# The opening of a two-block transformer kernel in another order: first product ahead of the context's norm, scalings in pairs, context's squares added by GpSimd

## What is computed

```python
mod_x = (silu(c) @ w_mod[i] + b_mod[i])[:, None, :]
mod_c = silu(c_ctx) @ w_mod[i] + b_mod[i]
sh_x, sc_x, g_x = jnp.split(mod_x, 3, axis=-1)
sh_c, sc_c, g_c = jnp.split(mod_c, 3, axis=-1)
hx = rms_norm(x, norm_g[i]) * (1.0 + sc_x) + sh_x
hc = rms_norm(ctx, norm_g[i]) * (1.0 + sc_c) + sh_c
```

## Time and profile before

| | before |
|---|---|
| median of three runs | 1638.76 us |
| the profiled execution | 1637.41 us |
| its span | 1635.7 us |
| PE busy | 1551.2 us (95%) |
| DVE, ACT, POOL busy | 740.2, 623.5, 658.7 us |
| mean granted clock of TensorE | 0.977 |

### The profile page before, as it was taken

One profiled execution on the slowest core, in us unless ns is written; L12 is line 12 of the kernel. 1 busy time (PEld: TensorE's weight loads), 2 busy tenths in 40 slices (PEclk: granted clock), 3 DMA queues, 4 the chain that ended last, 5 costly groups with the idle time before them and its releaser, 6 DMA issues.

```text
span 1635.7 us, 25366 instructions
## 1 busy us (share of the span) xinstructions
PE 1551.2 (95%) x10018; PEld 1227.2 (75%) x10018; DVE 740.2 (45%) x1717; ACT 623.5 (38%) x1303; POOL 658.7 (40%) x640
## 2 busy tenths in 40 slices
PE   5999999999898999999998899999999999999997
PEld 3887777787687888787876687878878865655755
DVE  4344555555533434444355563443424454456033
ACT  4234444454532533334344453433322343333221
POOL 2534344444432533434344453525345344333252
PEclk8999999999899999999999899999999999999998
DMA  9111111110133222323231222212122212110221
GB/s 396 47 60 52 31 49 53 53 52 27 72 123 103 78 78 78 104 78 110 72 104 52 78 92 73 100 52 103 52 78 78 90 66 78 52 52 27 78 98 57
DMA packets 22438, 129.80 MB, mean 79 GB/s; under 512 B 2480, under 2 KB 2608, under 8 KB 8368
## 3 DMA queue, kind: packets, MB, share of 16 engines
q1 hardware_dynamic: 22176, 127.92, 21.9%
q10 hardware_dynamic: 144, 0.26, 0.1%
HBM read 126.08 MB, written 2.10 MB: 78 GB/s over the span
## 4 chain that ended last, share of the span: by engine, by line
PE 81%; DVE 8%; ACT 3%; POOL 3%; issue 3%; DMA 1%; SPq 0%; POOLq 0%; DVEq 0%; ACTq 0%
PE PS L1442 15%; PE PS L1444 14%; PE PS L1443 14%; PE PS L1565 6%; PE PS L1540 6%; PE PS L1523 4%; PE PS L1696 3%; PE PS L1437 3%; PE PS L1438 3%; PE PS L1439 3%; PE PS L1530 3%; DVE sm L2154 2%; PE PS L1706 2%; PE PS L1618 1%; PE PS L1610 1%
## 5 line engine op out<-in xcount | busy, mean ns | idle before, releaser
L2477 POOL TENSOR_TENSOR WL<-W,WH 128x512 fp32r<-128x512 f32 x280 | 367.4, 1328 | 321.7 <-ACT WH L1726 321.4
L1442 PE MATMUL PS<-HX,WH 128*128 128x512 f32 x1008 | 420.5, 417 | 11.3 <-DVE LX L2067 3.7
L1444 PE MATMUL PS<-HX,WL 128*128 128x512 f32 x1008 | 398.6, 395 | 0.0
L1443 PE MATMUL PS<-LX,WH 128*128 128x512 f32 x1008 | 398.3, 395 | 0.0
L1442 PEld LDWEIGHTS PS<-HX,WH 128*128 128x128 f32 x1008 | 192.5, 191 | 62.7 <-issue 17.9
L1444 PEld LDWEIGHTS PS<-HX,WL 128*128 128x128 f32 x1008 | 192.1, 191 | 42.7
L1443 PEld LDWEIGHTS PS<-LX,WH 128*128 128x128 f32 x1008 | 192.7, 191 | 36.7 <-issue 3.4
L1726 ACT CAST WH<-W 128x512 fp32r<-128x512 f32 x296 | 172.0, 618 | 51.6 <-PE PS L1439 23.7
L1814 ACT ACTIVATE AR<-PS,sm 128x768 f32<-128x768 f32 (+4 forms) x160 | 115.7, 723 | 173.8 <-DVE sm L2159 101.1
L2154 DVE TENSOR_REDUCE sm<-PS 128x1 f32<-128x512 f32 (+4 forms) x224 | 149.9, 669 | 44.8 <-PE PS L1530 40.3
L2544 POOL TENSOR_SCALAR AR<-AR,sm 128x768 f32<-128x768 f32 (+1 forms) x96 | 77.1, 804 | 186.8 <-DVE sm L2170 186.8
(11 more groups left out here) (278 smaller groups left out, 2539.5 us busy)
## 6 DMA issues: line engine op xcount, KB each, us to landing
W<-in_wu SPq DMA_DIRECT2D x98, 1024.0 KB, 4.8
AR<-in_wu SPq DMA_DIRECT2D x8, 1024.0 KB, 11.2
AR<-in_biasb SPq DMA_DIRECT2D x32, 256.0 KB, 2.7
XX<-in_xt SPq DMA_DIRECT2D x2, 1024.0 KB, 6.1
out<-XX SPq DMA_DIRECT2D x8, 256.0 KB, 2.2
XX<-in_xt SPq DMA_DIRECT2D x2, 768.0 KB, 5.3
XC<-in_xt SPq DMA_DIRECT2D x1, 1024.0 KB, 14.3
C<-in_cc SPq DMA_DIRECT2D x1, 770.5 KB, 8.6
```

The source lines that it names most:

```text
L1442: e.matmul(o, wh, xh, start=(k == 0), stop=False)
L1443: e.matmul(o, wh, xl, start=False, stop=False)
L1444: t = e.matmul(o, wl, xh, start=False, stop=(k == 7))
L2477: e.tensor_tensor(WL[:, d, a:z], W[:, n % 2, a:z], WH[:, d, a:z].bitcast(F32), ALU.subtract).then_inc(*s_wl_pool.by(n, q))
```

## The change

Only the opening is rewritten.

1. **Loads.** XX arrives in three pieces (a quarter, a quarter, a half) on semaphores of their own, and weight unit 0 is loaded ahead of the context.
2. **First factors first.** The products and turns of the first two early units and the first `gain` stand ahead of everything of the context's norm. `rbroad` is divided into `rdiag` (VectorE, for all tokens of the part) and `rspread` (TensorE).
3. **The key products of chunks 0 and 1** stand ahead of the turns of early units 2 and 3; in every turn of the loop, x's products come ahead of the context's, and the context's follow two turns later.
4. **Pairs.** Both scalings of a turn stand ahead of both low parts.
5. **The context's squares** go to a buffer of their own for each chunk, so ScalarE need not wait for the additions, and GpSimd adds them (seven additions). They stand after x's first two chunks.
6. **The context's scaling.** GpSimd only multiplies by the norm (`norm_ctx_k`); ScalarE applies factor and shift twice from the same source, once rounded to the high part, once in full (`low_ctx_k`); GpSimd subtracts.
7. **Weight unit 0**: the low parts of its first two quarters are made by GpSimd.

```diff
-        norm("a", ar, X_CTX, (), lambda k, p: [(s_x[2], (2,)) if p else (s_x[k // 4], (k // 4,))])
+        norm("a", ar, X_CTX, (), lambda k, p: [(s_x[3], (3,))] if p else [(s_x[min(k // 2, 2)], (min(k // 2, 2),))])
+        norms["a"].apart = hb0
...
         norm_sums("a", 0, FIRST)
         next(first[0])
         do("norm_rs", "a", 0)
+        next(first[1])
         WIDE.take("RA", (s_scaled, (0, 7)), (s_rc, (0,)))
-        rbroad("a", 0, PS[:, 0:1024])
-        for k in range(KC):
-            do("square", "a", k, 1)
-        next(first[1])
-        norm_sums("a", 1, FIRST)
+        rdiag("a", 0)
+        split(0)
+        helped[0] = True
+        tick(True)
+        tick(True)
+        helped[0] = False
         run(first[0])
         run(first[1])
+        rspread("a", 0, PS[:, 0:1024])
...
-        split(0)
+        un = Unit("ak", whole=False)
         for n in range(0, 8, 2):
             do("gain", 0, n)
-            modulate_x(0, n)
-            if n == 0:
-                do("norm_rs", "a", 1)
-                tick(True)
-            modulate_x(0, n + 1)
+            do("scale", 0, n)
+            do("scale", 0, n + 1)
+            if n == 2:
+                rbroad("a", 1, PS[:, 0:1024])
+                do("scale_ctx", 0)
+            do("scale_low", 0, n)
+            do("scale_low", 0, n + 1)
             if n < 6:
                 next(first[n + 2])
+                if n == 0:
+                    for k in range(4):
+                        do("square", "a", k, 1)
                 next(first[n + 3])
-            if n == 0:
-                rbroad("a", 1, PS[:, 0:1024])
-                do("scale_ctx", 0)
-                un = Unit("ak")
-            else:
-                keys_rows(1, [n - 2, n - 1])
-            do("scale_ctx_k", 0, n)
-            do("scale_ctx_k", 0, n + 1)
+                if n == 0:
+                    for k in range(4, 8):
+                        do("square", "a", k, 1)
+            if n:
+                do("norm_ctx_k", 0, n - 2)
+                do("norm_ctx_k", 0, n - 1)
+            if n > 2:
+                do("low_ctx_k", 0, n - 4)
+                do("low_ctx_k", 0, n - 3)
+            keys_rows(0, [n, n + 1])
+            if n > 2:
+                keys_rows(1, [n - 4, n - 3])
+            tick(True)
+            if n > 2:
+                tick(True)
             if n < 6:
                 run(first[n + 2])
                 run(first[n + 3])
-            keys_rows(0, [n, n + 1])
-        keys_rows(1, [6, 7])
+            if n == 0:
+                norm_sums("a", 1, MODS)
+                do("norm_rs", "a", 1)
+        for k in (6, 7):
+            do("norm_ctx_k", 0, k)
+        for n in (4, 6):
+            do("low_ctx_k", 0, n)
+            do("low_ctx_k", 0, n + 1)
+            keys_rows(1, [n, n + 1])
...
+            def square(name, k, p):
+                N = norms[name]
+                if k and p and N.apart:
+                    lo, hi = 128 * N.parts[p][0], 128 * N.parts[p][1]
+                    w.wait_ge(*s_sq(name, k, p))
+                    if k > 1:
+                        w.wait_ge(*s_acc_pool(name, k - 1, p))
+                    e.tensor_tensor(N.acc[:, lo:hi], N.acc[:, lo:hi], N.apart.at(k, lo, hi), ALU.add).then_inc(*s_acc_pool.by(name, k, p))
...
-                for i in range(2):
-                    e.dma_start(XX[:, 2048 * i:2048 * i + 2048], xt[:, 2048 * i:2048 * i + 2048]).then_inc(*s_x[i].by(i))
+                for i, (a, b) in enumerate(((0, 1024), (1024, 2048), (2048, 4096))):
+                    e.dma_start(XX[:, a:b], xt[:, a:b]).then_inc(*s_x[i].by(i))
```

More of the change, by code:

```diff
@@ L248, in build @@
         s_v, s_c, s_cs, s_pos, s_out = (signal(n, 16) for n in ("vectors", "consts", "rope_table", "positions", "stored"))
-        s_x = [signal(f"x{i}", 16) for i in range(3)]
+        s_x = [signal(f"x{i}", 16) for i in range(4)]
         s_w = [signal(f"unit{i}", 16) for i in range(2)]
@@ L332, in build @@
         loaded, unit_end, split_by, split_prev, started = set(), {}, {}, {}, set()
-        pieces, quick, used, part_last = [], [False], [0], [None, None]
+        pieces, quick, helped, used, part_last = [], [False], [False], [0], [None, None]
         groups = {}
@@ L353, in tick @@
                 n, q = pieces.pop(0)
-                split_by[n, q] = "pool" if n > 1 and not quick[0] else "dve"
+                split_by[n, q] = "pool" if (n > 1 or helped[0]) and not quick[0] else "dve"
                 do("split", n, q)
@@ L371, in build, with __init__ @@
         class Unit:
-            def __init__(self, *key):
+            def __init__(self, *key, whole=True):
                 n = self.n = used[0]
@@ L380, in __init__ @@
                     split(n)
-                while any(m <= n for m, _ in pieces):
+                while whole and any(m <= n for m, _ in pieces):
                     tick(True)
@@ L451, in build, with added @@
             sums: object
+            apart: object = None
+            def added(self, name, k, p):
+                return (s_acc_pool if p and self.apart else s_acc)(name, k, p)
         norms = {}
@@ L474, in rbroad, with rdiag, rspread @@
         def rbroad(name, p, o):
+            rdiag(name, p)
+            rspread(name, p, o)
+        def rdiag(name, p):
+            for i in range(*norms[name].parts[p]):
+                dg_prev[name, i], dg_last[i % 4] = dg_last[i % 4], (name, i)
+                do("rdiag", name, i)
+        def rspread(name, p, o):
             rbout[name] = o
             for i in range(*norms[name].parts[p]):
-                dg_prev[name, i], dg_last[i % 4] = dg_last[i % 4], (name, i)
                 do("rbroad", name, i)
@@ L520, in build @@
         do("early", 1)
+        load(0)
         do("context_load")
-        load(0)
         for n in range(2, 8):
@@ L1739, in square @@
                 await_all(w, N.first)
-                if k > 2:
-                    w.wait_ge(*s_acc(name, k - 2, p))
-                o = N.acc if k == 0 else N.sq[(k - 1) % 2]
+                if p and N.apart:
+                    o = N.acc[:, lo:hi] if k == 0 else N.apart.at(k, lo, hi)
+                else:
+                    if k > 2:
+                        w.wait_ge(*s_acc(name, k - 2, p))
+                    o = (N.acc if k == 0 else N.sq[(k - 1) % 2])[:, lo:hi]
                 scale = 1.0 if N.gain is None else v(N.gain, k, k + 1)
-                e.activation(o[:, lo:hi], xT.at(k, lo, hi), ACT.Square, scale=scale).then_inc(*s_sq.by(name, k, p))
+                e.activation(o, xT.at(k, lo, hi), ACT.Square, scale=scale).then_inc(*s_sq.by(name, k, p))
             def scale_ctx(l):
@@ L2010, in square @@
                 lo, hi = 128 * N.parts[p][0], 128 * N.parts[p][1]
-                if k:
+                if k and not (p and N.apart):
                     w.wait_ge(*s_sq(name, k, p))
```

30 lines of the change are left out of this document (8 added, 22 removed).

## The result

The changed kernel takes 1641.47 us (median of 20 executions, 1638.43 to 1646.2) against 1638.76 for the kernel before on the same chip (20 executions, 1637.42 to 1641.87): the ratio is 1.0018, with a 95% interval of 1.0011 to 1.0024. That is 2.9 us slower (1.8 to 3.9), with 0.18% inside the 0.2% that the prediction calls "the same" (the interval reaches 0.24%), and 1.8 us above the 1639.7 that it names.

A forecast was written before the change was run, and what follows sets the result against it. TensorE bounds the kernel, so only the last key matmul's end counts: 4.5 us won, 1.5 lost, 2.6 won, then context work at the end, 0.9 us later: 1639.7 us, range 1635.7 to 1642.6.

The forecast's parts named there:

- the sum: Whole opening: 4.5 us won, 1.5 given back, 2.6 won again, context work moved to the end; keys end 0.9 later.
- To the first product: Opening up to the first key product: it starts at 27.5, 4.5 us earlier than 31.98, set by early unit 3's load.
- rival 4: Opening loads: smaller XX pieces make loads late, the first product gains 2 us and not 4.5; 1642.2 us, 8% chance.
- To the second group: First to second group of key products: start at 38.9, 3.0 us ahead of before, so 1.5 of the 4.5 lost.
- Rival 2: Key products of x: one more group, first or third, at half rate; 1641.4 or 1642.2 us, 20% chance.
- Rival 3: Context's sums: GpSimd's additions become the wait, ending at 35.1, 2.8 us later; 1642.5 us, 7% chance.
- To the third and the fourth group: Later key groups: third starts at 45.7, 5.6 us ahead of before; fourth at 53.9 behind 2.9 us of TensorE idle.
- Rival 1: Fourth group and early units 4 and 5: no half rate there, time 1637.2 down to 1635.7 us, 20% chance.
- To the end: Fourth group at half rate, 5.4 us, then 36 context matmuls, 4.3, ScalarE's passes covered: keys end at 63.9, 0.9 later.
- Pairs: Scalings and low parts of two chunks: 3.0 us from first scaling to second low part, sharing 2.6 won at third group.
- signs for "wrong": Keys' end at 61 or below or above 66, sums not waiting for GpSimd's additions, or a larger difference behind the keys.
- signs for "right": First key product at 27 to 28, later groups at about 39 and 46, last key matmul ending at 63 to 65.

The follow-up runs named there:

- e1: Changed kernel with XX loaded in two halves again instead of three pieces: median 1639.72 us, ratio 1.0010 to the kernel before.
- e2: Kernel before with XX loaded in three pieces, nothing else: median 1640.74 us, ratio 1.0014 to the kernel before.
- e3: Changed kernel with the seven additions of the context's squares on VectorE instead of GpSimd: median 1640.11 us, ratio 1.0013 to the kernel before.
- e9: Changed kernel with three of four pairs undone, each low part right behind its scaling: median 1645.72 us, ratio 1.0047 to the kernel before.
- e10: Changed kernel with XX in two pieces and the context's additions on VectorE: median 1638.71 us, ratio 1.0003 to the kernel before.
- e4: Changed kernel with 52 matmuls nobody reads in TensorE's two idle stretches: median 1639.12 us, ratio 1.0005 to the kernel before.
- e5: Changed kernel with XX in two pieces, additions on VectorE and unread matmuls in the idle stretches: median 1638.32 us, ratio 0.9989 to the kernel before.
- e6: Kernel before with the pairs alone, both scalings ahead of both low parts: median 1636.38 us, ratio 0.9980 to the kernel before.
- e8: Changed kernel with the whole opening reordered, XX in two pieces, additions and the context's second scaling on VectorE: median 1634.66 us, ratio 0.9966 to the kernel before.
- e7: Kernel before with six unread 128x128 matmuls ahead of the spread of the context's norm: median 1640.34 us, ratio 1.0006 to the kernel before.

## Why the prediction was right, and where not

The range, 1635.7 to 1642.6, held the time, "within 0.2%" was right, and so was the shape: a gain at the first product that is lost before the last key. But the loss was three times the 0.9 us of the sum, and two of its steps failed: the loads, and the price of the pairs. That the time still lies in the range is in part luck. In the profile the keys ended at 67.99, 4.1 later than forecast and beyond the 66 that the prediction names as a sign of a wrong step. Had the median moved by the whole 5.0 us of the keys it would be 1643.8, outside the range; it moved by 2.7.

- **To the first product: wrong by 2.0.** The forecast had the second half of XX "stay" at 8.8 and early unit 3 at 25.6; they came at 10.9 and 27.8, and the first product started at 29.54 and not 27.5. This is rival 4, which had 8% and named the right mechanism and nearly the right place ("gains 2 and not 4.5": it gained 2.4). e1 and e2 show it, and with two pieces the first product starts at 27.55 to 27.67, as forecast. The step that failed counted bytes in the queue and not the rate that smaller pieces reach. The forecast's turns were too short as well (1.0; at half rate they took 1.87), but the load covers that.
- **To the second group: right in kind, 1.5 more late.** It started at 42.45, predicted 38.9. Of the 3.55, 2.0 are the load. The additions took 0.92 each in place of 0.84, 0.5 in all, and ended at 34.83; the early units were wholly at half rate, 3.64 and not 2.8, 0.8 more; the rest is 0.2. The idle time ahead of the spread (1.61 and 2.18) was foreseen as "most of 31.5 to 35.4". Rival 2, the first group at half rate, did not come in this profile (3.05 us), but in part in those of e3, e9 and e10.
- **Rival 3, GpSimd's additions as the wait,** came true in a small way: 1.61 us of idle time ends with them, most of it because the squares began 2 us late with unit 2. One addition, at 31.94, took 1.16 us, the median is 0.74; VectorE's only instruction with two SBUF inputs in that stretch, a low part of weights, ran from 31.82 to 32.51. The mechanism of 1.24 in the earlier trace rows thus struck once in seven. The Trainium skill (SBUF — State Buffer, "SBUF: two separate sides") has this as a lock held for the whole instruction; by it one collision in this stretch is what to expect, and the trace agrees in that. Of the VectorE instruction 0.57 us were left when the addition began, and the addition took 0.42 more than the median.
- **To the third and the fourth group: right.** From the second group's start to the third's it was 7.2 (predicted 6.8), from there to the fourth's 8.7 (8.2). The idle stretch ahead of the fourth was 3.15 (2.9), and the half rate behind it 5.4 (5.4). Rival 1 fell.
- **To the end: right, for a narrow reason.** The 36 context matmuls took 4.3, and ScalarE's two passes (0.6 each) were covered, though they ran from 58.0 to 64.8 and not from 54 to 59. e4 and e5 show what covers them: the half rate of the fourth group. Without it the context's chain through ScalarE and GpSimd costs 1.4 us. So rival 1's 2.5 us could not have been had in full.
- **Pairs: mis-sized.** The forecast gave the pairs a share in the 2.6 us won at the third group, and called them covered at the first. e9 and e6 put them at 4.8 and 3.3 us, the largest single gain that a run of this case gives to one part of the change (the intervals are wide, 1.5 to 5.1 for e6). Put the other way round, the change without three of its four pairs was 7.7 us slower than before (e9), and the pairs without the rest 3.3 us faster (e6).
- **The profile against the median.** The forecast added 0.9 to both; the profiled executions differ by 4.8 and the medians by 2.7. One profile does not show why. The time of an execution goes with its mean granted clock (last section), so the place of the lower clock, which varies from run to run, is the likely reason; it is not shown for the opening.

Of the signs for "wrong" that the prediction named one came: the keys' end above 66 said that a step was off. The first product at 29.54, outside the 27 to 28 of the signs for "right", said which to look at first. The other two did not come: the sums waited for GpSimd's additions, and behind the keys the two profiles differ by 0.2 us.

## What to carry to other kernels

Where an engine hands a chunk to a second one and takes it back (scale, shift and round, subtract), issue the hand-overs of two chunks ahead of both takings-back; here it cost nothing at the first chunk (48.76 against 48.78), and took a wait of 0.79 us per chunk away, also for what stood behind on the partner. Splitting a first load to start sooner has to be priced by the rate in the windows behind it, since the later transfers of the queue pay. And a reordering that moves work out of idle stretches to the end can lose twice, once by its length and once by the clock behind the stretch: in e4's profile 3.4 us came back at the keys by filling the stretches with work that nobody needs. e8, which puts needed work there, is the fastest of all, but it has other edits too.

## What the runs showed that was not expected

- Two transfers of 512 KB in place of one of 1 MB lowered the rate of the queue from 346 and 421 to 295 and 330 GB/s in the windows from 2 to 5 and 5 to 8 us, with the DMA engines as busy (0.94 to 1.02). The first drop came in all five profiles with three pieces, the second in full in three (e4 had 384, e3 419).
- The granted clock does not show the slow stretch at the start. Every profile has 1.00 there from the first us, while TensorE's first matmuls take the times of 1.2 GHz. In the changed kernel a pair of early units takes 3.64 us (at 46.44 one takes 1.93):

```profile
16.58 3.64 PE L1492 MATMUL PS<-AR,sm 128*32 128x256 f32 x32
```
```profile
16.00:20.00 4.00, 4.00 (x36) 1.92 (x35) 1.04 (x5) 0.37 (x1) 1.01 (x1) 1.00 1.01 426
```

  In e8 this lasts longest: seven matmuls of 128x512 took 0.62 to 0.77 us, and the next ones 0.39 to 0.43, while the granted clock was 1.00 in the windows that hold them (28 to 32, and this one):

```profile
32.98 0.62 PE L1503 MATMUL PS<-HX,WH 128*128 128x512 f32 x1
...
33.67 0.40 PE L1505 MATMUL PS<-HX,WL 128*128 128x512 f32 x1
```
```profile
32.00:36.00 4.00, 4.00 (x34) 2.62 (x37) 2.41 (x5) 1.12 (x3) 0.53 (x1) 1.00 0.99 408
```

- With one idle stretch filled the lower clock came at another group (e7), and with both long ones filled at none of x's (e4). The stretch from 1280 to 1320, far behind the opening, had 1.00 in the profiles of before, after and seven others, 0.96 in e7's, and 0.91 in those of e2, e6 and e8. Whether the edits have to do with it one profile each cannot show, but from the keys' end to the end these four took 2.3 to 4.3 us longer than before's 1572.7, so the time of such a profile says less of the edit than its opening does.
- The time of an execution goes with its mean granted clock. Of the 20 executions of the changed kernel, the six with 0.969 or 0.970 took 1643.15 to 1646.2 us, the eleven with 0.977 to 0.980 took 1638.43 to 1642.21.
